# The first two modulation vectors by channel quarters, folded on TensorE, with the norm of x on VectorE

## The reference

```
cond = silu(c)
mod = cond @ ada_w[i] + ada_b[i]              # 1024 -> 6 * 1024
shift1, scale1, gate1, shift2, scale2, gate2 = split(mod, 6)
h = rmsnorm(x, norm1_g[i]) * (1.0 + scale1) + shift1
qkv = h @ a_w_qkv                             # 1024 -> 3072
...                                           # attention, w_o, gate1, then the feed-forward part
```

## Time and profile before

| | us |
|---|---|
| runs | 1041.74, 1040.72, 1043.99 |
| median | 1041.74 |
| profiled execution, first to last instruction | 1033.8 |
| TensorE busy | 986.3 (95%) |
| VectorE busy | 740.2 (72%) |
| ScalarE busy | 542.6 (52%) |

### The profile page before, as it was taken

One profiled execution on the slowest core, in us unless ns is written; L12 is line 12 of the kernel. 1 busy time (PEld: TensorE's weight loads), 2 busy tenths in 40 slices (PEclk: granted clock), 3 DMA queues, 4 the chain that ended last, 5 costly groups with the idle time before them and its releaser, 6 DMA issues.

```text
span 1033.8 us, 13550 instructions
## 1 busy us (share of the span) xinstructions
PE 986.3 (95%) x5102; PEld 827.2 (80%) x5102; DVE 740.2 (72%) x1053; ACT 542.6 (52%) x875; POOL 68.4 (7%) x126
## 2 busy tenths in 40 slices
PE   2999799999999999999999999999999999999997
PEld 2887577888878787778888886888888779999986
DVE  5988888878877897887665447647753777777643
ACT  4466846544443485575444436575546474444442
POOL 2100222000000411010000002000000010000000
PEclk8999999999999999999999999999999999999999
DMA  9998167998889472449865553856444367656551
GB/s 339 371 371 285 39 204 230 344 321 295 273 304 359 162 250 101 143 127 321 263 203 186 183 184 108 269 160 205 134 142 143 119 190 218 187 177 189 184 184 41
DMA packets 126968, 219.89 MB, mean 213 GB/s; under 512 B 9235, under 2 KB 78088, under 8 KB 126904
## 3 DMA queue, kind: packets, MB, share of 16 engines
q1 hardware_dynamic: 125200, 215.52, 63.4%
q0 software_dynamic: 1088, 2.87, 0.8%
q10 hardware_dynamic: 616, 0.65, 0.2%
HBM read 217.96 MB, written 1.05 MB: 212 GB/s over the span
## 4 chain that ended last, share of the span: by engine, by line
PE 84%; DVE 8%; ACT 4%; issue 2%; DMA 1%; POOL 0%; SPq 0%; POOLq 0%; DVEq 0%; ACTq 0%
PE bank L1900 13%; PE bank L1902 13%; PE bank L1901 13%; PE bank L1913 5%; PE bank L1915 5%; PE bank L1914 5%; PE bank L2504 3%; PE bank L2505 3%; PE bank L2506 3%; DVE w_lo L1156 2%; PE bank L1961 2%; PE bank L1963 2%; PE bank L1962 2%; ACT w_hi L638 1%; DVE ada_acc L1186 1%
## 5 line engine op out<-in xcount | busy, mean ns | idle before, releaser
L1156 DVE TENSOR_TENSOR w_lo<-raw,w_hi 128x1024 fp32r<-128x1024 f32 x312 | 379.1, 1223 | 215.3 <-ACT w_hi L638 214.5
L638 ACT ACTIVATE w_hi<-raw 128x1024 fp32r<-128x1024 f32 x312 | 328.2, 1061 | 338.4 <-PE bank L1902 139.7
L1900 PE MATMUL bank<-w_hi,h_hi 128*128 128x512 f32 x608 | 244.3, 402 | 3.7 <-DVE w_lo L1156 3.7
L1902 PE MATMUL bank<-w_hi,h_lo 128*128 128x512 f32 x608 | 238.3, 392 | 0.0
L1901 PE MATMUL bank<-w_lo,h_hi 128*128 128x512 f32 x608 | 237.9, 391 | 0.0
L1900 PEld LDWEIGHTS bank<-w_hi,h_hi 128*128 128x128 f32 x608 | 114.8, 189 | 28.4 <-issue 6.1
L1902 PEld LDWEIGHTS bank<-w_hi,h_lo 128*128 128x128 f32 x608 | 114.7, 189 | 24.6
L1901 PEld LDWEIGHTS bank<-w_lo,h_hi 128*128 128x128 f32 x608 | 114.9, 189 | 23.6 <-issue 1.0
L2504 PE MATMUL bank<-h_hi,w_hi 128*128 128x256 f32 x320 | 90.8, 284 | 1.1 <-DVE conv_t L1828 1.1
L2505 PE MATMUL bank<-h_hi,w_lo 128*128 128x256 f32 x320 | 90.7, 283 | 0.0
L2506 PE MATMUL bank<-h_lo,w_hi 128*128 128x256 f32 x320 | 90.7, 283 | 0.0
(11 more groups left out here) (328 smaller groups left out, 1372.2 us busy)
## 6 DMA issues: line engine op xcount, KB each, us to landing
raw<-in_f_w_in SPq DMA_DIRECT2D x176, 256.0 KB
ada<-in_ada_w SPq DMA_DIRECT2D x86, 512.0 KB, 5.9
raw<-in_w_in SPq DMA_DIRECT2D x46, 512.0 KB
raw<-in_f_w_out SPq DMA_DIRECT2D x44, 512.0 KB
raw<-in_w_up SPq DMA_DIRECT2D x88, 256.0 KB
raw<-in_a_w_qkv SPq DMA_DIRECT2D x24, 512.0 KB
raw<-in_w_down SPq DMA_DIRECT2D x22, 512.0 KB
raw<-in_b_w_qkv SPq DMA_DIRECT2D x12, 512.0 KB
```

The costliest lines, as they stand in the source:

```text
L638: nc.scalar.activation(w_hi[:, m % SPL], raw[:, m % RAW], ACT.Copy).then_inc(hi_done, 1)
L1156: ve.tensor_tensor(w_lo[:, m % SPL], raw[:, m % RAW], w_hi[:, m % SPL].bitcast(F32), ALU.subtract).then_inc(lo_done, 1)
L1900: mm(o, hi, w_hi[:, s, k], start=(u == 0 and k == 0), stop=False)
L1902: last = mm(o, lo, w_hi[:, s, k], start=False, stop=(u == 3 and k == 1))
```

## The change

It loads x first, and then ada_w for vectors 0 and 1 by quarters of the channels (`load_quarter`: a tile has 256 channels of shift and of scale for two rows k, in two transfers with rows of 1 KB). TensorE folds them (`fold_quarter`): four matmuls a tile, each with a weight of 32 columns of which only the first is filled with cond, each writing another 32 partitions of bank 6. After four tiles VectorE copies the four sums (`take_rows`), TensorE adds and turns them (`column_sums`, with `sel`), and VectorE makes a quarter of mod, gains and h (`modulate(q)`). The first twelve weight tiles go by quarter, three chunks each. VectorE squares and scales x. Folds of tiles 16 on are placed anew, and AHEAD and the marks for emptying the banks with them. A `...` stands for lines left out.

```diff
-TILES_A = [(c, u) for u0 in (0, 2) for c in range(3) for u in (u0, u0 + 1)] + [(c, u) for c in range(3, 6) for u in range(4)]
+TILES_A = [(c, u) for u in range(4) for c in range(3)] + [(c, u) for c in range(3, 6) for u in range(4)]
...
-CHUNK_DONE_A = {7: 0, 9: 1, 11: 2, 15: 3, 19: 4, 23: 5}
+CHUNK_DONE_A = {9: 0, 10: 1, 11: 2, 15: 3, 19: 4, 23: 5}
...
+QUARTERS = 4
+FIRST_LOADS = "aaaa0a1aa2a34a5aaa67aa8aa9"
...
-    after = dict(zip(range(16, 36), (8, 9, 10, 11, 12, 14, 15, 16, 18, 19, 20, 22, 23, 24, 26, 27, 28, 28, 29, 29)))
-    after.update({36: 31, 37: 31, 38: 31, 39: 31})
+    after = dict(zip(range(16, 36), (11, 12, 12, 13, 14, 15, 16, 17, 18, 20, 20, 21, 22, 22, 23, 24, 26, 27, 28, 28)))
+    after.update({36: 29, 37: 29, 38: 31, 39: 31})
...
-LOAD_BEFORE = {**FOLD_AFTER, 33: 29, 34: 30, 35: 31, 36: 32, 37: 32, 38: 33, 39: 33}
+LOAD_BEFORE = {**FOLD_AFTER, 33: 28, 34: 29, 35: 30, 36: 31, 37: 32, 38: 33, 39: 33}
...
-LEAD, LEAD_EV, AHEAD = 3, 2, 2
+LEAD, LEAD_EV, AHEAD = 3, 2, 4
...
+        rows = ada_acc[:, 0, 0:HC]
...
+                if a in (18, 19):
+                    sp.wait_ge(quarter_fold, a - ADA_SLOTS + 1)
+                if a >= 20:
+                    sp.wait_ge(ada_done, a - 16 - ADA_SLOTS + 1)
...
+            def load_quarter(a):
+                q, r = divmod(a, 4)
+                tile, arrived, _ = ada_tile(a)
                 if a in (14, 15):
-                    sp.wait_ge(ada_done, a - 14 + 3)
-                if a >= 18:
-                    sp.wait_ge(ada_done, a - ADA_SLOTS + 1)
-                if a < 16:
-                    src = ada_w[0][k * P:(k + 1) * P, 0:2 * D].rearrange("p (v h n) -> p h v n", v=2, h=2)[:, g]
-                else:
-                    src = ada_w[layer][k * P:(k + 1) * P, j * D:(j + 1) * D].rearrange("p (a n) -> p a n", a=2)
-                sp.dma_start(tile, src).then_inc(arrived, 16)
+                    sp.wait_ge(quarter_fold, a - 14 + 3)
+                for par in range(2):
+                    k = 2 * r + par
+                    src = ada_w[0][k * P:(k + 1) * P, 0:2 * D].rearrange("p (v q n) -> p q v n", v=2, q=QUARTERS)[:, q]
+                    sp.dma_start(tile[:, par].rearrange("p (v n) -> p v n", v=2), src).then_inc(arrived, 16)
...
-            for a in range(2):
-                load_ada(a)
             for t in range(T):
-                sp.dma_start(x[:, t], x_in[0, t * P:(t + 1) * P, :]).then_inc(x_load, 16)
-            for a in range(2, 9):
-                load_ada(a)
-            for m in range(4):
-                load_a(m)
-            for a in range(9, 14):
-                load_ada(a)
-            load_a(4)
-            load_ada(14)
-            load_a(5)
-            load_ada(15)
-            for m in range(6, 24):
+                sp.dma_start(x[:, t], x_in[0, t * P:(t + 1) * P, :]).then_inc((x_load0, x_load1)[t], 16)
+            first_quarters = 0
+            for what in FIRST_LOADS:
+                if what == "a":
+                    load_quarter(first_quarters)
+                    first_quarters += 1
+                else:
+                    load_a(int(what))
+            for m in range(10, 24):
                 load_a(m)
...
+            nc.gpsimd.memset(cond_cols[:], 0.0).then_inc(cond_ok, 1)
+            nc.gpsimd.memset(sel[:], 0.0).then_inc(sel_ok, 1)
+            for j in range(4):
+                pool.wait_ge(sel_ok, j + 1)
+                nc.gpsimd.memset(sel[32 * j:32 * j + 1, j % 2:j % 2 + 1], 1.0).then_inc(sel_ok, 1)
+            pool.wait_ge(sel_ok, 5)
...
-            pool.wait_ge(ada_done, 8)
+            pool.wait_ge(quarter_fold, 12)
...
-            pool.wait_ge(ada_done, 12)
+            pool.wait_ge(quarter_fold, 14)
...
-            square(0)
-            square(1)
-            scale(0)
-            scale(1)
             for kk in range(4):
                 act.wait_ge(t_done, kk + 1)
-                nc.scalar.activation(hf[:, 2 * kk:2 * kk + 2], bank[4 + kk][:].rearrange("p (k s) -> p k s", k=2),
+                nc.scalar.activation(hf[:, 2 * kk:2 * kk + 2], bank[2 + kk][:].rearrange("p (k s) -> p k s", k=2),
                                      ACT.Copy).then_inc(raw_x, 1)
...
             split(0)
             high_0(0)
+            for m in range(1, 4):
+                split(m)
             high_0(1)
-            for m in range(1, SPL + AHEAD):
+            for m in range(4, 7):
                 split(m)
             high_0(2)
+            for m in range(7, SPL + AHEAD):
+                split(m)
             high_0(3)
...
+            def spread_cond():
+                v_.wait_ge(cond_ok, 1)
+                ve.tensor_copy(cond_cols[:, :, 0], cond[:]).then_inc(cond_ok, 1)
+            def square(t):
+                v_.wait_ge((x_load0, x_load1)[t], 16)
+                ve.tensor_tensor_reduce(out=hf[:, 4 * t:4 * t + 4].rearrange("p k s -> p (k s)"), in0=x[:, t], in1=x[:, t],
+                                        scale=1.0, scalar=0.0, op0=ALU.mult, op1=ALU.add,
+                                        accum_out=stat[:, SS + t:SS + t + 1]).then_inc((sq0, sq1)[t], 1)
+            def scale(t):
+                v_.wait_ge(rstd_ok, t + 1)
+                ve.tensor_scalar(xn[:, t], x[:, t], stat[:, RSTD + t:RSTD + t + 1], None, ALU.mult).then_inc((xn0, xn1)[t], 1)
+            def take_rows(q):
+                v_.wait_ge(quarter_fold, 4 * q + 4)
+                if q:
+                    v_.wait_ge(quarter_mm, q)
+                ve.tensor_copy(rows, bank[6][:, 0:HC]).then_inc(quarter_rows, 1)
+            def modulate(q):
+                v_.wait_ge(quarter_mm, q + 1)
...
+                part = lambda row, first: row[:, first:first + 16].rearrange("p (v k) -> p v k", v=2)[:, :, 2 * q:2 * q + 2]
+                ve.tensor_tensor(part(mod, 0), bank[7][:, 4 * q:4 * q + 4].rearrange("p (v n) -> p v n", v=2),
+                                 part(vecs, ADAB_V), ALU.add).then_inc(quarter_mod, 1)
+                v_.wait_ge(quarter_mod, q + 1)
+                ve.scalar_tensor_tensor(out=gains[:, 2 * q:2 * q + 2], in0=mod[:, 8 + 2 * q:10 + 2 * q], scalar=1.0,
+                                        in1=vecs[:, N1_V + 2 * q:N1_V + 2 * q + 2], op0=ALU.add,
                                         op1=ALU.mult).then_inc(gain_ok, 1)
+                v_.wait_ge(gain_ok, q + 1)
+                v_.wait_ge(raw_x, q + 1)
+                for k in (2 * q, 2 * q + 1):
+                    last = ve.tensor_scalar(hf_mod[:, k % 4], hf[:, k], gains[:, k:k + 1], mod[:, k:k + 1],
+                                            ALU.mult, ALU.add)
+                last.then_inc(hf_ok, 1)
+                if q == 0:
+                    low(0)
+                v_.wait_ge(hf_ok, q + 1)
+                v_.wait_ge(h_hi_ok, q + 1)
+                ve.tensor_tensor(h_lo[:, 2 * q:2 * q + 2], hf_mod[:, 2 * q % 4:2 * q % 4 + 2],
+                                 h_hi[:, 2 * q:2 * q + 2].bitcast(F32), ALU.subtract).then_inc(h_lo_ok, 1)
...
+            spread_cond()
+            square(0)
+            square(1)
+            scale(0)
+            scale(1)
+            take_rows(0)
             v_.wait_ge(setup, 2)
             modulate(0)
             low(1)
             low(2)
-            fold(9)
-            fold(10)
+            take_rows(1)
             low(3)
-            fold(11)
-            fold(12)
+            modulate(1)
             low(4)
-            for a in range(13, 16):
-                fold(a)
             low(5)
-            low(SPL)
-            modulate(1)
+            take_rows(2)
+            low(6)
+            modulate(2)
+            low(7)
+            low(8)
+            take_rows(3)
+            low(9)
+            modulate(3)
...
-            for m in range(21):
+            for m in range(AHEAD, 21):
...
-                if m == 10:
+                if m == 12:
...
+            def turn_x(t):
+                pe.wait_ge((xn0, xn1)[t], 1)
+                for kk in range(4):
+                    for k in range(2):
+                        last = nc.tensor.transpose(bank[2 + kk][:, k * S + t * P:k * S + (t + 1) * P],
+                                                   xn[:, t, (2 * kk + k) * P:(2 * kk + k + 1) * P], ident[:])
+                    if t == T - 1:
+                        last.then_inc(t_done, 1)
+            def fold_quarter(a):
+                q, r = divmod(a, 4)
+                tile, arrived, count = ada_tile(a)
+                pe.wait_ge(arrived, count)
+                if r == 0 and q:
+                    pe.wait_ge(quarter_rows, q)
+                for par in range(2):
+                    for v in range(2):
+                        j = 2 * par + v
+                        last = mm(bank[6][32 * j:32 * j + 32, 0:HC], cond_cols[:, 2 * r + par], tile[:, par, v * HC:(v + 1) * HC],
+                                  start=(r == 0), stop=(r == 3))
+                last.then_inc(quarter_fold, 1)
+            def column_sums(q):
```

(56 more changed lines are left out.)

107 lines of the change are left out of this document (40 added, 67 removed).

## The result

| | kernel before | changed kernel |
|---|---|---|
| median of 19 runs each | 1040.45 us | 1044.6 us |
| lowest and highest | 1037.7, 1043.99 | 1041.96, 1047.46 |
| profiled execution, span | 1033.8 | 1043.3 |

The changed kernel is slower: the ratio is 1.0047, 95% interval 1.0037 to 1.0056, so 4.9 us (3.8 to 5.8). That is past the 0.3% that I count as no change. The time lies in my range (1037.0 to 1050.5), but in the case to which I gave 0.30, not in the likeliest. One execution of all those timed here, 1117.97 us of the kernel before in its second profiling, was in a slower state and is left out of the ratios.

The account below looks back on a forecast made before the run. TensorE was taken as the bound. Terms −6.3 + 6.5 + 1.35 − 1.7 + 3.35 + 0.75 − 2.75 gave +1.2 us on the 1033.8 span, 1035.0; with 7.9 from span to median, 1042.9 us, range 1037.0 to 1050.5.

Parts of the forecast that it names:

- Start, −6.3: Program start: first weight tile on TensorE at 19.4 instead of 25.69 us, 6.3 us earlier.
- Folds +6.5: After the first tile: eleven folds (5 to 15) now stand between weight tiles on TensorE, adding 6.5 us.
- sums +1.35: After the first tile: three more column sums on TensorE, 0.45 us each, adding 1.35 us.
- waits +3.35: Before tiles 3, 6 and 9: TensorE waits for copies and for each quarter's mod and h, adding 3.35 us.
- reduce −1.7: After the first tile: reduce_vector(1) on TensorE goes away, saving 1.7 us.
- Pairwise and serial folds: Rival, every fold: groups overlap only two at a time (7.3 us on top) or not at all (21.8); chance 0.18.
- Rope +0.75: After tiles 9 to 12: VectorE turns the queries later than TensorE wants them, adding 0.75 us.
- The rest of the stage stays: Tile 9 to the scores, 47.3 us: unchanged apart from the rope wait, VectorE's slack there mostly used.
- SP's order stays fed ... all at nothing: Load queues: weight tiles land ahead of need, and SP's and GpSimd's waits for fold 14 are covered; cost nothing.
- Boundary −2.75: At reduce_vector(4): two folds moved ahead of low(31) remove TensorE's wait and the half clock after it, saving 2.75 us.
- the boundary gives nothing: Rival at reduce_vector(4): VectorE arrives late by other work and TensorE stands again, 2.75 us on top; chance 0.12.
- the slower case: Whole kernel: slower than forecast, through folds not four at a time or a boundary without gain; chance 0.30.

Follow-up runs that it names:

- loads: Changed kernel with ada_w tiles 18 to 32 loaded one or two weight tiles later in SP's list; ratio 1.0024 to the kernel before.
- turns: Changed kernel with folds 5 to 15 in three earlier groups, column sums a whole tile ahead, VectorE's copy and modulate one place earlier; ratio 1.0021 to the kernel before.
- serial: Changed kernel with all but folds 0, 4, 8 and 12 of the first sixteen writing to one group of 32 partitions; ratio 1.0199 to the kernel before, median 1060.98 us.
- boundary3: Kernel before with folds 32 to 37 after low 27, 28, 28, 29, 29, 30, loads of 31 to 38 one place later than boundary2; ratio 0.9991, median 1037.7 us.
- warm: Changed kernel with 16 extra 128x128 matmuls on TensorE before the first fold; ratio 1.0042 to the kernel before, median 1042.68 us.
- together: Changed kernel with the edits of loads and turns plus five 128x256 filler matmuls before the first weight tile; ratio 0.9971 to the kernel before, median 1036.63 us.
- together2: The kernel of together with low(6) ahead of modulate(2) and low(9) ahead of modulate(3) in VectorE's list; ratio 0.9971 to the kernel before.
- boundary2: Kernel before with folds 32 to 37 after low 27, 28, 28, 29, 29, 30 and their loads moved earlier with them; ratio 1.0035 to the kernel before.

## Why the prediction was right or wrong

**Start, −6.3.** Measured −5.4 to the first profile of before, −6.5 to the second. The order in which I put the limits (TensorE at half clock up to fold 2, not VectorE's norm) is what the rows show: after 8.40 it has no wait before the sums. Of the 0.9 between 19.4 and 20.32, 0.4 is there when fold 0 ends (it starts at 8.40) and 0.6 comes from the second eight transposes, all at half clock, where I had let the clock rise in the middle. `loads` and `turns`, which start with the same instructions, have tile 0 at 19.95 and 19.71, so part of it is one execution's luck.

**Folds +6.5, sums +1.35, waits +3.35, reduce −1.7.** From tile 0 to 9 I had 9.5 more, measured 37.81 − 29.13 = 8.7. What each tile start is later than twelve matmuls (2.73) is the price: one fold 0.83 (tile 3 to 4), two 1.21 and 1.26, three 1.65, fold with sum and copy wait 1.89, sum and turn 1.70 and 1.71. I had 0.73, 1.16, 1.59, 1.73, 1.65, so nearly every term was a little low. What makes the measured sum smaller all the same is a term that I did not have, 0.7: the clock in tile 0, at half for eight matmuls instead of eleven. "Tile 9 near 57" was a slip against my own terms: 54.82 − 6.3 + 9.5 is 58.0, and it came at 58.13. Pairwise and serial folds are excluded, by the serial run.

**Rope +0.75.** Measured 1.36 and 0.3 of hand-over. Part of it (0.45) is SP's queue, by the `loads` run (0.91 is left); the rest I put down to VectorE's own row of work, which no run takes out.

**"The rest of the stage stays", "SP's order stays fed ... all at nothing".** This is the step that failed. I followed SP's wait for fold 14 before ada tile 18 and found cover for it, but looked at no later load. The new table folds tiles 25 and 26 both after low(20), and ada 29, loaded before weight tile 22, needs fold 25. The kernel before had fold 25 after low(19) and that load before weight tile 24. ScalarE's 13.5 us of waits for transfers, TensorE's 0.46 and 2.11, and part of the rope wait come from such places: 2.4 us in the time, by the run that moved loads alone. "If this cover is gone, each microsecond counts" was right, and nothing was priced for it.

**Boundary −2.75.** Measured −2.46 (offset +7.96 at the first product with w_o, +5.50 at the first feed-forward product). Right in size, but "two of four folds move ahead" was not enough of a reason: that edit alone costs 3.2 us, because four folds then come in a row; with those of 32 and 34 moved as well and the loads left late (boundary3), the trace gains 1.2. The rival "the boundary gives nothing" had more behind it than the 0.12 it got.

**The sum and the distance.** +1.2 was forecast behind the boundary, +5.5 measured. Step by step, rounded: 0.9 at the start, −0.8 in the folds, 0.5 between tiles 9 and 12 (0.35 of it four transposes of w_sp, which moved behind tile 11), 0.9 at the rope, 0.5 and 1.9 at scores and softmax, 0.3 at the boundary. The distance of 7.9 between span and median was no constant of the program: the profiled execution was one of the shortest, and where span and own time are both recorded the distance is 1.73 to 1.89. The 1042.9 came nearer to 1044.6 than the working deserved, as three runs of before had a median 1.3 above that of nineteen. And the slower case came true by luck: its 0.30 was made of folds that are not four at a time and of a boundary that gives nothing, and neither happened. What made the kernel slower, SP's queue and VectorE's lateness between tile 9 and w_o, was in no rival.

## What to carry to other kernels

When a table of loads and folds is shifted, walk the issuing queue over the whole stage, not only at the first wait: for each load ask what frees its slot and what is issued behind it. An early part can gain 5 us (tile 0 here) and the kernel be slower all the same, when later waits take more. A gain at the front of one profile need not show in the median (the warm run), and one profile of it does not tell why. An edit that works inside a change need not work alone. Profile the reference twice before comparing spans to within 1%.

## What the runs showed of the hardware

Four matmuls of 32 output columns each, to four groups of 32 partitions, ran fully side by side: 0.43 us for eight records against 1.73 with all four sent to one group, a factor of 4.0. The Trainium skill ("TensorE: Matmul & The Clock Gate", Part 3: Packing small matmuls) has 3.07 for four row groups and 2.38 for three column groups; these folds lost nothing.

Half clock did not follow from the waits alone. Behind the same waits of about 2.5 and 1.5 us in the softmax the granted clock of 106 to 115 us was full in one kernel and lower in the next. First together, then together2, with the clock third from the end:

```profile
106.00:115.00 9.00, 5.76 (x46) 4.72 (x47) 7.43 (x21) 7.77 (x33) 1.11 (x3) 1.00 0.21 86
```
```profile
106.00:115.00 9.00, 6.83 (x41) 5.43 (x42) 5.85 (x17) 6.21 (x26) 1.11 (x3) 0.81 0.02 7
```

It costs 1.6 us in `loads` (8.3 instead of 6.7 between two softmax steps), and half clock was there in the softmax in seven of fourteen profiles, `serial` and `boundary2` with its longer wait among them. What decides it stays open; it is enough to hide or fake a gain of this size in a single profile. At the program's start it varies as well (the reduction, 2.70 and 3.57 in the same program). The Trainium skill ("TensorE: Matmul & The Clock Gate", Part 1: The HAM clock gate) says that the number of matmuls at half clock differs from run to run of one kernel; these rows agree.

The stretch of 4 to 20 us, whose ada_w tiles now come in rows of 1 KB, moved less in the same share of DMA time, 355 GB/s against 386 before, 8%; the 1 KB rows of the feed-forward weights in the earlier trace rows had led me to 374. No run changes the length of the rows alone. The stretch in the changed kernel:

```profile
4.00:20.00 16.00, 8.82 (x63) 4.95 (x63) 6.93 (x13) 5.41 (x9) 3.41 (x5) 1.00 1.05 355
```
